# Projecting the memory keys and values ahead of everything else instead of inside the first attention loop

## What is computed

```python
# first block
mod = jax.nn.silu(cvec) @ w_mod + b_mod              # six parts of 1024 columns
hx = modulate(rmsnorm(x, norm1_g), sh1, sc1)         # the same for the context
qa, ka, va, qb, kb, vb = split_proj(hx @ w_in)
...
x = x + g1 * (jnp.concatenate([ya, yb], axis=-1) @ w_out)
hx2 = modulate(rmsnorm(x, norm2_g), sh2, sc2)
x = x + g2 * moe(hx2, ...)                           # 32 experts, 12 MB of weights each
# second block
kv_me = rmsnorm_2(mem, norm_mem) @ w_mem_kv          # 1024 x 1024 weights
k_me, v_me = kv_me[..., :512], kv_me[..., 512:]
o_me = memory_attention(q_me, k_me, v_me)
```

## Time and profile before

| | |
|---|---|
| median of 3 runs | 1701.89 us (1701.84 to 1705.04) |
| the profiled execution | 1704.64 us, its span 1702.8 us |
| PE busy | 1586.2 us (93%) |
| DVE busy | 542.3 us (32%) |
| ACT busy | 435.3 us (26%) |
| HBM read | 522.72 MB, mean 308 GB/s over the span |
| chain that ended last | PE 59%, DMA 34%, DVE 3%, ACT 2% |

### The profile page before, as it was taken

One profiled execution on the slowest core, in us unless ns is written; L12 is line 12 of the kernel. 1 busy time (PEld: TensorE's weight loads), 2 busy tenths in 40 slices (PEclk: granted clock), 3 DMA queues, 4 the chain that ended last, 5 costly groups with the idle time before them and its releaser, 6 DMA issues.

```text
span 1702.8 us, 23717 instructions
## 1 busy us (share of the span) xinstructions
PE 1586.2 (93%) x10016; PEld 977.8 (57%) x10016; DVE 542.3 (32%) x1089; ACT 435.3 (26%) x849; POOL 7.2 (0%) x16
## 2 busy tenths in 40 slices
PE   5999999999999999999999999998699999899997
PEld 3786776443343333334333433333299988789997
DVE  3755513110101010110101010101255474477863
ACT  3433622010001010101101100000445552456542
POOL 0000000000000000000000000000000100000000
PEclk9999998999999999999999999999999999999999
DMA  9325736999999999999999999999734624425420
GB/s 393 152 80 221 294 119 250 433 431 432 432 431 431 431 431 431 431 433 434 433 433 432 433 431 432 431 432 431 299 116 157 186 99 149 149 99 198 175 99 25
DMA packets 27432, 524.79 MB, mean 308 GB/s; under 512 B 2931, under 2 KB 7027, under 8 KB 7492
## 3 DMA queue, kind: packets, MB, share of 16 engines
q1 hardware_dynamic: 24368, 519.06, 73.2%
q10 hardware_dynamic: 2484, 3.19, 0.7%
q0 software_dynamic: 512, 1.57, 0.4%
HBM read 522.72 MB, written 1.08 MB: 308 GB/s over the span
## 4 chain that ended last, share of the span: by engine, by line
PE 59%; DMA 34%; DVE 3%; ACT 2%; issue 1%; SPq 0%; ACTq 0%; DVEq 0%
PE ps L596 58%; DMA ring<-in_w_down 33%; PE ps L724 1%; DMA arena<-in_ctxT 1%; DMA ring<-in_first 1%; DVE ring_r L1641 0%; DVE arena L1623 0%; PE ps L1078 0%; DVE nrm L1620 0%; ACT w_high L1448 0%; DVE hx_lo L1648 0%; DVE arena L1654 0%; DVE arena L1955 0%; ACT L1191 0%; ACT arena L1198 0%
## 5 line engine op out<-in xcount | busy, mean ns | idle before, releaser
L596 PE MATMUL ps<-ring,arena 128*64 128x512 f32 (+1 forms) x3872 | 721.6, 532 | 45.4 <-DMA ring<-in_w_down 31.2
L596 PEld LDWEIGHTS ps<-ring,arena 128*64 128x64 f32 (+1 forms) x3872 | 240.3, 132 | 478.1 <-issue 403.4
L596 PE MATMUL ps<-arena_r,w_high 128*128 128x256 f32 x1840 | 339.5, 287 | 10.2 <-DVE arena_r L1935 9.4
L596 PEld LDWEIGHTS ps<-arena_r,w_high 128*128 128x128 f32 x1840 | 289.8, 193 | 15.0 <-issue 12.2
L596 PE MATMUL ps<-arena 128*128 128x128 f32 (+5 forms) x1780 | 262.4, 379 | 6.8 <-DVE arena L1838 1.6
L596 PE MATMUL ps<-arena_r,ring_r 128*128 128x256 f32 x920 | 261.7, 284 | 0.0
L1862 DVE TENSOR_SCALAR arena<-ps 128x512 f32<-128x512 f32 x32 | 22.1, 692 | 716.4 <-PE ps L596 716.4
L596 PEld LDWEIGHTS ps<-arena 64*128 64x128 f32 (+3 forms) x1780 | 167.5, 176 | 112.1 <-issue 98.1
L596 PEld LDWEIGHTS ps<-arena_r,ring_r 128*128 128x128 f32 x920 | 178.2, 194 | 0.0
L1909 DVE TENSOR_TENSOR ring_r<-ring,w_high 128x1024 fp32r<-128x1024 f32 x120 | 142.0, 1221 | 102.4 <-ACT w_high L1448 102.4
L1448 ACT ACTIVATE w_high<-ring 128x1024 fp32r<-128x1024 f32 x120 | 120.8, 1054 | 26.4 <-PE ps L596 26.4
(11 more groups left out here) (203 smaller groups left out, 1052.2 us busy)
## 6 DMA issues: line engine op xcount, KB each, us to landing
ring<-in_w_gate_up SPq DMA_DIRECT2D x64, 4096.0 KB, 20.8
ring<-in_w_down SPq DMA_DIRECT2D x32, 4096.0 KB, 19.7
ring<-in_second SPq DMA_DIRECT2D x32, 2048.0 KB, 8.2
ring<-in_first SPq DMA_DIRECT2D x19, 2048.0 KB, 12.5
ring<-in_first SPq DMA_DIRECT2D x3, 1024.0 KB, 5.1
ring<-in_second SPq DMA_DIRECT2D x2, 1024.0 KB, 5.0
small<-in_small ACTq DMA_DIRECT2D x1, 1024.5 KB, 8.3
arena<-in_xT SPq DMA_DIRECT2D x1, 1024.0 KB, 8.1
```

The source lines that it names most:

```text
L596: return nc.tensor.matmul(out_, lhsT, rhs, start=start, stop=stop, **kw)
```

## The change

The memory comes first in everything. SP loads `memT` ahead of `x` and the context. The keys' half of `w_mem_kv_2` (512 columns, `KEYS`) goes into slot 4, which is not used by the first stage any more. The values' half is a unit between the third and fourth of `w_mod` in `FIRST`. PE does the sums of squares of the memory first, then those of `x`, then both key jobs, three modulation rows, a value job, the fourth row, the other value job, and only then `project(0)`. The results are copied by ACT into a buffer of their own (`k_me1`, `v_me1`), and POOL moves them to their old place after the attention loop. The modulation rows are now the fillers of steps 5 to 12, and steps 13 to 17 have none. `memory_job(3)` before the router is gone. All units of `FIRST` go round in slots 0 to 3. The first pair of expert weights (slots 4 and 5) is issued after unit `U_MOD2 + 1`, when the job `vb` is done, ahead of six modulation units. `scale1` is made in two halves, since its second half needs the fourth row.

```diff
-FIRST = [blocks("w_mod", 512 * u, 512) for u in range(4)]
+KEYS = blocks("w_mem_kv_2", 0, 512)
+FIRST = [blocks("w_mod", 512 * u, 512) for u in range(3)]
+U_KV = len(FIRST)
+FIRST += [blocks("w_mem_kv_2", 512, 512), blocks("w_mod", 512 * 3, 512)]
 U_IN = len(FIRST)
 FIRST += [blocks("w_in", 512 * u, 512) for u in range(4)] + [blocks("w_in", 2048, 256)]
-U_KV = len(FIRST)
-FIRST += [blocks("w_mem_kv_2", 0, 256), blocks("w_mem_kv_2", 512, 512)]
 U_MOD2 = len(FIRST)
 FIRST += [blocks("w_mod", 512 * u, 512) for u in range(4, 12)]
 U_OUT = len(FIRST)
 FIRST += [blocks("w_out", 512 * u, 512) for u in range(2)]
-U_KV2 = len(FIRST)
-FIRST += [blocks("w_mem_kv_2", 256, 256)]
...
-        KV_STEP = len(JOBS) - EARLY
-        ADA_STEP = KV_STEP + 3
+        ADA_STEP = len(JOBS) - EARLY
...
-        freed = [(ada_mm, n + 1) for n in range(4)]
+        freed = [(ada_mm, n + 1) for n in range(3)] + [(kv_mm, 4), (ada_mm, 4)]
...
+            sp.dma_start(memT, io["memT"]).then_inc(mem_in, 16)
             sp.dma_start(xT, io["xT"]).then_inc(x_in, 16)
             sp.dma_start(hx[:, :, T:2 * T], io["ctxT"]).then_inc(ctx_in, 16)
+            sp.dma_start(ring[:, SLOT_KEYS, :], keys).then_inc(slot_full[SLOT_KEYS], 16)
             for u, src in enumerate(first):
-                if u == U_IN + 4:
-                    sp.dma_start(memT, io["memT"]).then_inc(mem_in, 16)
-                load(u, unit_dst(SLOT_1[u], src), src)
-                if u == U_OUT:
-                    for at in (PAIRS[0], PAIRS[0] + 1):
-                        sp.wait_ge(*freed[last_in(at)])
+                load(u, unit_dst(u % RING1, src), src)
+                if u == U_MOD2 + 1:
+                    sp.wait_ge(proj_mm, JOBS.index(("vb", 0)) + 1)
                     pair_of(0, w_gu[0, 0], slot_full)
...
+            pool.wait_ge(proj_mm, len(JOBS))
+            pool.wait_ge(kv_act, 4)
+            nc.gpsimd.tensor_copy(k_me, k_me1).then_inc(kv_moved, 1)
+            nc.gpsimd.tensor_copy(v_me, v_me1).then_inc(kv_moved, 1)
...
-            sum_squares(NORM1, sq, 7, 2 * T)
+            sum_squares(NORM_MEM, sq_m, 7, T)
+            sum_squares(NORM1, sq, 6, 2 * T)
...
+            memory_job(0)
+            memory_job(1)
             pe.wait_ge(cs_set, 1)
-            for n in range(4):
+            for n in range(3):
                 ada_rows(n, 5)
                 ada_turn(n, COL_BANKS[n])
+            memory_job(2)
+            ada_rows(3, 5)
+            ada_turn(3, COL_BANKS[3])
+            memory_job(3)
...
             def project(n):
                 name, i = JOBS[n]
+                if n < 2:
+                    pe.wait_ge(kv_act, n + 3)
...
-            memory_job(3)
             for t in range(TT):
...
+            for k in range(KC // 2):
+                normed_hi(k)
+            copy_memory(2)
+            ada_copy(3, 5)
+            split_hi1(0)
+            for k in range(KC // 2, KC):
+                normed_hi(k)
+            copy_memory(3)
             for p in range(1, HI_PARTS):
                 split_hi1(p)
...
+            for n in range(3):
+                ada_columns(n, COL_BANKS[n])
+            scales(0)
+            for half in range(2):
+                for k in range(KC // 2):
+                    modulated(k, half)
+            for k in range(KC // 2):
+                normed_lo(k, 0)
+            ada_columns(3, COL_BANKS[3])
+            scales(1)
+            for k in range(KC // 2, KC):
                 modulated(k, 0)
             split_lo1(0)
-            for k in range(KC):
+            for k in range(KC // 2, KC):
                 normed_lo(k, 0)
...
             split_lo1(1)
-            for k in range(KC):
+            for k in range(KC // 2, KC):
                 modulated(k, 1)
```

More of the change, by code:

```diff
@@ L328, in build @@
         w_gu, w_dn = io["w_gate_up"], io["w_down"]
-        first, second = units("first", FIRST), units("second", SECOND)
+        (keys, *first), second = units("first", [KEYS, *FIRST]), units("second", SECOND)
         def unit_dst(index, src):
             return ring[:, index, 0:src.shape[1]]
[L334 to L337, removed]
         def filled(u):
-            return 16 * SLOT_1[:u + 1].count(SLOT_1[u])
+            return 16 * (u // RING1 + 1)
         def fills1(at):
-            return SLOT_1.count(at)
-        def last_in(at):
-            return max(u for u in range(U_MOE) if SLOT_1[u] == at)
+            return len(range(at, U_MOE, RING1)) if at < RING1 else int(at == SLOT_KEYS)
         def filled_c(c):
@@ L473, in step_c @@
             return kind, j, qt, (T if kind == 2 else P * (qt + 1)), (1 if kind == 2 else 2)
-        NORM1, NORM_MEM, NORM2, NORM_MIX, NORM_POST, NORM_FFN, NORM_LAST = range(7)
+        NORM_MEM, NORM1, NORM2, NORM_MIX, NORM_POST, NORM_FFN, NORM_LAST = range(7)
         def chain(engine, done):
@@ L502, in load @@
             def load(u, dst, src):
[L503 to L508, removed]
+                if u >= RING1:
+                    sp.wait_ge(*freed[u - RING1])
+                sp.dma_start(dst, src).then_inc(slot_full[u % RING1], 16)
             def pair_of(q, src, full):
@@ L1206, in _ @@
             load_table(ACT.Sqrt)
+            act.wait_ge(mem_in, 16)
+            for k in range(KC):
+                square(NORM_MEM, k, sq_m[:, k % 2], memT[:, k])
+            root(NORM_MEM, 7)
             act.wait_ge(x_in, 16)
@@ L1224, in ada_copy @@
                 A(modrow[:, n % 2], ps[:, bank, 0:P], ACT.Copy).then_inc(ada_row, 1)
-            for n in range(4):
+            copy_memory(0)
+            copy_memory(1)
+            for n in range(3):
                 ada_copy(n, 5)
@@ L1279, in _ @@
                     act.dma_start(bias_rows.ap().rearrange("(g h) n -> h g n", g=2), brow[0:8]).then_inc(bias_out, 16)
-                if MEM_JOB <= n < MEM_JOB + 4:
-                    act.wait_ge(mem_in, 16)
-                    for k in range(2 * (n - MEM_JOB), 2 * (n - MEM_JOB) + 2):
-                        square(NORM_MEM, k, sq_m[:, k % 2], memT[:, k])
-                if n == MEM_JOB + 4:
-                    root(NORM_MEM, 7)
             act.wait_ge(lam_set, 1)
@@ L1606, in _ @@
             neg_lam = lamv[:, 1:2]
-            dve.wait_ge(root_set, 1)
-            link(V.reciprocal(r1, rope1))
-            for k in range(KC):
-                V.tensor_tensor(hx[:, k, 0:T], xT[:, k], r1[:, 0:T], ALU.mult)
-                last = V.tensor_tensor(hx[:, k, T:2 * T], hx[:, k, T:2 * T], r1[:, T:2 * T], ALU.mult)
-            link(last)
             rinv = nrm[:, 0]
@@ L1623, in times @@
                 return V.scalar_tensor_tensor(dst, src, g, rinv, ALU.mult, ALU.mult)
+            inverse_rms(NORM_MEM)
+            for k in range(KC):
+                times(memT[:, k], memT[:, k], col("mem_g")[:, k:k + 1]).then_inc(mem_set, 1)
+            dve.wait_ge(root_set, NORM1 + 1)
+            link(V.reciprocal(r1, rope1))
+            for k in range(KC):
+                V.tensor_tensor(hx[:, k, 0:T], xT[:, k], r1[:, 0:T], ALU.mult)
+                last = V.tensor_tensor(hx[:, k, T:2 * T], hx[:, k, T:2 * T], r1[:, T:2 * T], ALU.mult)
+            link(last)
             def ada_columns(n, bank):
@@ L1706, in _ @@
                 rope(n)
-                if n == MEM_JOB + 4:
-                    inverse_rms(NORM_MEM)
-                    for k in range(KC):
-                        times(memT[:, k], memT[:, k], col("mem_g")[:, k:k + 1]).then_inc(mem_set, 1)
             def maxima(a):
@@ L2166 @@
     weights["w_ffn_up_2"] = x["w_ffn_up_2"].reshape(D, 2, FC // 2, 2 * P).transpose(0, 2, 1, 3).reshape(D, -1)
-    arrays["first"], arrays["second"] = laid_out(FIRST, weights), laid_out(SECOND, weights)
+    arrays["first"], arrays["second"] = laid_out([KEYS, *FIRST], weights), laid_out(SECOND, weights)
     arrays["b_gate_up"], arrays["b_down"] = x["b_gate_up"], x["b_down"]
```

130 lines of the change are left out of this document (59 added, 71 removed).

## The result

The changed kernel takes 1710.93 us (median of 4 runs, 1709.35 to 1713.38), the kernel before on the same chip 1701.87 us (4 runs). The ratio is 1.0052, interval [1.0032, 1.0072]: slower by 9 us, where I had said 1702.0 with 1695.5 to 1707.5 as the range. Executions of one and the same kernel differ: the four of before lie between 1700.8 and 1705.0 us, and 57 more of it, run beside the experiments, between 1700.3 and 1711.5 us.

A forecast was written before the change was run, and what follows sets the result against it. The prediction took a first stage, mostly dense PE work, to set when a fixed-length experts block begins. Terms +19.1 - 2.8 - 18.2 + 2.2 - 0.3 summed to 0.0 us: 1702 us, range 1695.5 to 1707.5.

The forecast's parts named there:

- What bounds the kernel: Whole kernel: the experts are a block of fixed length, so each microsecond of the first stage (0 to 271 us) passes on whole.
- The keys are in by some 20 us, so the two key jobs run to 38.9 us: At the start: key jobs follow the squares of x, which end at 25.1 us, at 6.9 us a job.
- the term: The start, up to the third projection job: forecast at 76.3 us against 57.2, so +19.1 us, upper end 23.
- cold start: Rival at the start: the array at its slower level in a key job, +3.5 us or more, 1706 us; 1 in 10.
- the memory's squares: At the start: the memory's sums of squares on PE take 6.0 us, from 9.4 to 15.4 us.
- the rows and the value jobs: At the start, after the key jobs: modulation rows at 2.61 us and value jobs at 6.9 us, from 38.9 to 63.1 us.
- the tail: From the last value job to the third projection job: a chain on ACT and DVE, summing to 12.9 us.
- transfers that keep ahead of PE: At the start: the fourth row's unit is in at 49 us, w_in's first at 54 us, before PE needs them.
- The projections: Between projection jobs: the memory's squares disappear, four times 0.67 us, so -2.8 us, upper bound 3.4.
- The loop: Attention loop, steps 5 to 16: 71.8 us becomes 53.6, -18.2 us, with 2.2 us back from late modulation rows.
- The rival on the pair: Attention loop: the expert pair holds up modulation rows, +6 us instead of +2.2, 1706 us; 2 in 10.
- Before the router: Ahead of the router: removing the key job gains 2.1 us, slow clock returns 1.8, so -0.3, ends -2.1 and +2.

The follow-up runs named there:

- start jobs cut: Changed kernel with seven eighths of the matmuls of all four memory jobs left out, loads, copies and norm kept: 1692.8 us, 0.9924 of the kernel before.
- both: Changed kernel with the memory's norm ahead of the csig product on VectorE and the first expert pair issued at the first w_out unit: 1699.02 us, ratio 0.9971.
- norm first: Changed kernel with the memory's norm put ahead of the csig product on VectorE, nothing else altered: 1702.93 us, 0.9984 of the kernel before.
- copy late: The version called both, with ScalarE's copy of the last value job put behind the three splits instead of ahead: 1697.94 us, 0.9971 of the kernel before.
- pair late: Changed kernel with the first expert pair issued at the first w_out unit rather than after unit U_MOD2 + 1: 1706.72 us, 1.0011 of the kernel before.
- router job cut: Kernel before the change, with seven eighths of the matmuls of its key job ahead of the router left out: 1702.21 us, ratio 0.9998.
- key job back: As copy late, but the second key job returns ahead of the router, its 1 MB of keys loaded behind w_out: 1692.93 us, 0.9938 of the kernel before.

## Why the prediction was wrong, step by step

**What bounds the kernel: right.** Whatever the first stage gains or loses was passed on whole: from the first expert's mark to the end of the span it is 1400.7 to 1403.9 us in all versions, a spread of 3.2 us that does not follow the versions: 1401.0 with the mark at 290.50 (start jobs cut), 1403.7 with it at 299.14 (before), 1403.9 with it at 297.27 (both).

**The step that failed: "The keys are in by some 20 us, so the two key jobs run to 38.9 us".** It begins the key jobs as soon as PE is through with the squares, at 25.1, and asks only whether the keys are in. It never asks when the memory's norm is ready, which is VectorE's work, and what is queued ahead of it there. The norm was ready to start at 15.8 us and started at 24.90. That costs 4.8 us by itself and 2.0 us by the clock behind the hole, 6.8 in all; the rest of the term stands, for norm first has the third job at 75.58 us against the 76.3 of my sum. I had a "cold start" among the rivals, at 3.5 us or more and without its cause. Norm first shows that the order on VectorE is the cause: with it changed, the key jobs begin 5.5 us earlier and the stretch at 1.2 GHz in them is gone.

**Right in the same term:** the memory's squares (6.2 us, forecast 6.0), the rows and the value jobs (45.7 to 69.94 is 24.2 us, forecast 24.2), the tail (13.0, forecast 12.9), and transfers that keep ahead of PE. That the tail's own order cost 2.1 us, as the copy late shows, the sum took as given.

**The projections: right**, -3.4 us, the upper bound that I gave.

**The loop: right mechanism, one size off.** Steps without a filler took 3.59, 3.41 and 3.70 us, forecast 3.65: an emptied PE meets ScalarE's pace. The pair was to cost 2.2 us and cost 4.3. The row's unit was in 18.6 us after the issue of the pair, not 17.2: the pair took 13.7 us to land, and 12.3 was the shortest of the earlier trace rows, far from the median of 17.9. The sum took a best case for the expected one, and the 11.6 us of the formula that the prediction quotes are further off still. The wait was 2.96 us instead of 1.8, the 0.4 us for the next rows did not come, and the row behind the wait took 1.3 us more at 1.2 GHz, which the sum did not have. The rival on the pair (+6 us) named this cause; it came to 4.3. Pair late shows that this whole cost was a matter of where SyncE issues.

**Before the router: right in kind, and in size partly by luck.** PE was to wait some 3 us there and waited 3.41; all 32 small matmuls of the router ran slow, not only the second half. The stage was 0.4 us shorter in after, its repetition, start jobs cut and the copy late, but 0.7 to 0.8 us longer in norm first, pair late, both and router job cut (0.8 us, from 56.1 to 56.9), where the stretch at 1.2 GHz is longer. Measured apart, the matmuls of a job there have no price that shows in the time (router job cut). The Trainium skill (TensorE: Matmul & The Clock Gate, HAM oscillation) says of idle gaps between bursts that they bring the half clock back; this trace agrees, with 6.92 us for 32 matmuls that took 3.65 us without a gap ahead of them.

**The sum.** 6.6 us at the start (82.94 less 76.3), 2.1 in the loop, less 0.6 in the projections and 0.1 before the router: 8.0 us. The first expert starts 7.65 us later.

**Where the gain of the change went.** Taking three jobs out of the loop and one from before the router is worth 18 us plus nothing (71.8 to 53.6 us in pair late), and 27.6 us of PE work goes into a place where PE of before had only some 10 us of holes (4.8 ahead of the first projection job, 3.3 between the first three, the rest at the modulation rows). With the two orders mended the same idea is 0.3% ahead of before by the ratio, 1.9 us by the first expert's mark: the projections are 3.4 us shorter, and the part from the first to the third of them 3.4 (17.0 to 13.6). With the one job put back that was free where it stood it is 0.6%.

**Open.** Why the stretch at 1.2 GHz ahead of the experts is 10.2 us long in one version and 20.5 or 23.9 in another is not settled, nor whether it belongs to the version or to the one profiled execution. It takes 1.2 us of what pair late gains in the loop and 1.8 of what both gains, and I could not have forecast it from the rows of before.

## What to carry to other kernels

When a job is moved to the front, list for each of its operands the engine that makes it, and read that engine's own order from the top: an instruction ahead of it that waits for something unrelated delays it as much as a missing transfer. Work that stands in a place where its engine waits anyway can be free there, as the key job ahead of the router was; moved to the start, which was short of bytes and of time, the same 6.9 us job cost 6.45 us at the third projection job, so move only what stands in dense stretches. And price a transfer that others queue behind by a range, not by its best landing: the pair landed after 13.7 us, between the best of its kind (12.3) and the median (17.9).

## What the runs showed of the hardware

- The hole of 5.6 us ahead of the key jobs brought 6.8 us at 1.2 GHz, half of them in the matmuls behind it, which took 15.8 us instead of 14.0. Pair late and start jobs cut, with the same hole, have the same 6.8 us; without the hole (norm first) there was none at that place.
- The 32 small matmuls of the router took 3.65 and 3.78 us in the two versions with a key job right ahead of them (before, key job back), and 6.9 to 7.0 us in those where PE waited 2.6 to 3.4 us there. From there to 300 us PE was granted 1.2 GHz for 10.2 us in all in the first two, for 17.0 to 23.9 us in the others.
- After and its repetition agree in all four stretches at 1.2 GHz to within half a microsecond. Yet these are not a fixed property of a program: before and router job cut have the same program up to 253 us, and at the first projection jobs the one has 3.4 us at 1.2 GHz (from some 40 us on), the other 10.2 us (from some 33 us on), where PE had waited 1.51 us instead of 0.31 for the load of the fourth modulation row. So part of the difference between single profiles, at the router too, can be chance; one profile of each version can't tell.
- A unit of 2 MB behind a lone pair of 4 MB was in 18.6 us after the pair's issue; the pair took 13.7 us (after, issued at 162.34 us, with no transfer under way in the 12 us before).
